# Rotary score passes of two heads on 64 rows each, and the order of copies around them, in a latent-attention layer on one NeuronCore

## Chip, cores and metric

The kernel runs on one core of a Trainium2 chip. The metric is the device time of one execution in microseconds (us); lower is better. Everything is computed in float32: each operand of a matmul is split into a high part (rounded to the matmul's format, `fp32r`) and a low part (what is left), and a product is made of hi x hi, hi x lo and lo x hi.

## What is computed

One decoder layer: multi-head latent attention, a residual with LayerNorm, a squared-ReLU MLP, and a second residual with LayerNorm. There are 512 tokens of width 2048, 16 heads, 128 plain and 64 rotary dimensions of queries and keys, 128 of values. The part that matters here:

```python
cq, ckv, k_rope = split(x @ w_in)                # 512, 512 and 64 wide
q = (rms_norm(cq) @ w_uq).reshape(B, S, 16, 128 + 64)
kv = (rms_norm(ckv) @ w_ukv).reshape(B, S, 16, 128 + 128)
q_rope, k_rope = apply_rope(q_rope), apply_rope(k_rope)   # one k_rope for all heads
s = (q_nope @ k_nope.T + q_rope @ k_rope.T) * 192 ** -0.5
p = softmax(where(causal, s, -inf))              # 128-query blocks
h = layer_norm(ALPHA * x + (p @ v) @ w_o)
```

## The kernel before

Every engine has its own instruction stream, written out by hand in a function of its own; semaphores tie them together, and the order within a stream is the order of the code. There is no scheduler. The stages follow one another: the input projection (up to 110 us of the trace), attention (to about 372), the output projection by Strassen-like products (to about 500), LayerNorm, and the MLP.

Attention goes by pairs of heads, `attention(pair, ahead)`, eight times; pair 0 and the last ones stand apart, the others run in a loop on each engine. While a pair's scores become probabilities, TensorE makes the projections of the next pair (`ahead`). For one pair TensorE runs: `scores` of head 0 and of head 1; `query` of the next pair's two heads and `rope_query`, the rotary queries of both heads (12 matmuls of 512 columns each); `transpose_probs` of head 0; `key` 0; `transpose_probs` of head 1; `key` 1 and `value` 0; `weigh_values` of both heads; `value` 1. The last pair has no next one: in place of the three projections stand `first_o_products`, 18 matmuls of the output projection.

`scores(pair, h)` makes, for each of four query blocks `t`, the scores against the 128 (t + 1) keys up to it, in the three banks of PSUM of head `h` (banks 0 to 2 for head 0, 3 to 5 for head 1). Five passes each: three of the plain part (`product`), then rotary with the key's high part (`kr_hi`), then with its low part (`kr_lo`). `qr[:, h, :]` holds the high part of head `h`'s rotary queries in 64 partitions (the first half for head 0, the second for head 1) and their low part in the other 64; `kr_hi` holds the key's high part in both halves, so that one pass adds hi x hi and lo x hi. `kr_lo[:, h, :]` holds the low part of the key in the half of head `h` and zeros in the other.

VectorE: `maxima` waits for a head's scores (`scored`), adds the causal mask, takes the row maxima and negates them; `normalise` divides by the sums; `query`, `key` and `values` make the low parts of the projections; `head_parts_lo` (L1536) makes `o_lo`, the low parts of the previous pair's seven sums of head outputs; `rope_query` rotates; `prob_t_los` makes the low parts of the transposed probabilities. ScalarE: `exps`, the copies out of PSUM that make the high parts (`q_hi`, `k_hi`, `v_hi`, `pt_hi`, `qr`), the swap of the rotary halves (`rope_swap`, L796), and `weights`, the high part of a block of weights. GpSimd makes the low part of that block (L666). A pair has four blocks of weights, held in four slots; each goes through one of two raw buffers, and SyncE loads a raw buffer when the low part of the block two before is made (L407).

The bank that `query(pair + 1, 0)` writes (6) is also that of `rope_query(pair + 1)`, which therefore waits until VectorE has made `q_lo` of head 0. `key(pair + 1, 0)` writes the bank of `query(pair + 1, 1)`.

Of the kernel before, what the change touches and what calls it, by code (L numbers as in the profile page):

```python
# [4 lines left out]
P = 128  # L5
D = 2048
S = 512
KD = D // P
TT = S // P
# [15 lines left out]
QKV_HB = 4  # L25
HB_QKV = IN_HB
# [66 lines left out]
KB = 1024  # L93
# [56 lines left out]
def mla_mlp_program(nc, xT, x, w, w_out, w_up, w_down, const, gain, ln, out):  # L150
# [3 lines left out]
    with ExitStack() as ctx:  # L154
# [33 lines left out]
        kr_hi, kr_lo = sb("kr_hi", [P, S], f32r), sb("kr_lo", [P, 2, S], f32r)  # L188
        place[0] += 2 * KB
# [547 lines left out]
        def _(act):  # L737
# [96 lines left out]
            def rope_query(pair, stream=True):  # L834
                if stream:
                    weights(HB_QKV + QKV_HB, pair)
                rope_swap(pair + 1, rope_bank(pair))

            def rope_query_hi(pair):
                act.wait_ge(rope_rotated, pair + 2)  # L840
                for half, h in zip(halves, range(2)):
                    last = act.activation(qr[half, h, :], rot[half, :], ACT.Copy)
                last.then_inc(rope_hi, 1)

# [68 lines left out]
            def attention(pair, ahead, stream=True):  # L913

                behind = not (isinstance(pair, int) and pair == 0)
                if behind:
                    head_parts_hi(pair - 1)
                    store_heads(pair - 1, 0)
                exps(pair, 0)
                if ahead:  # L920
                    query(pair + 1, 0)
                exps(pair, 1)
                if ahead:
                    query(pair + 1, 1)
                    rope_query(pair + 1, stream)
                else:
                    o_weights(0, 2)
                prob_t_his(pair, 0)
                if ahead:
                    key(pair + 1, 0)  # L930
                    rope_query_hi(pair + 1)
                else:
                    store_heads(pair - 1, 1)
# [408 lines left out]
        def _(dve):  # L1342
# [64 lines left out]
            for h in range(2):  # L1407
                last = dve.memset(kr_lo[64 - 64 * h:128 - 64 * h, h, :].bitcast(f32), 0.0)
            last.then_inc(ones_made, 1)
# [53 lines left out]
            def key_rope_lo():  # L1463
                dve.wait_ge(rope_hi, 1)
                dve.wait_ge(ones_made, 2)
                for half, h in zip(halves, range(2)):
                    last = dve.tensor_tensor(kr_lo[half, h, :], rot[half, :], kr_hi[half, :].bitcast(f32), ALU.subtract)
                last.then_inc(rope_split, 1)
# [122 lines left out]
            def attention(pair, ahead):  # L1591

                behind = not (isinstance(pair, int) and pair == 0)
                maxima(pair, 0)
                maxima(pair, 1)
                normalise(pair, 0)
                if ahead:
                    query(pair + 1, 0)
                else:
                    head_parts_lo(pair - 1)  # L1600
                normalise(pair, 1)
                if ahead:
                    query(pair + 1, 1)
                    if behind:
                        head_parts_lo(pair - 1)
                    rope_query(pair + 1)
                    key(pair + 1, 0)
# [564 lines left out]
        def _(pe):  # L2172
# [158 lines left out]

            def scores(pair, h):
# [5 lines left out]
                for t in range(TT):  # L2338
                    q, keys = slice(P * t, P * t + P), slice(0, P * (t + 1))
                    dst = score_bank(h)[:, SCORE_AT[t]:SCORE_AT[t] + P * (t + 1)]  # L2340
                    product(dst, q_hi[:, h, q], q_lo[:, h, q], k_hi[:, h, keys], k_lo[:, h, keys], True, False)

                    pe.matmul(dst, qr[:, h, q], kr_hi[:, keys], start=False, stop=False)  # L2343

                    last = pe.matmul(dst, qr[:, h, q], kr_lo[:, h, keys], start=False, stop=True)  # L2345
                last.then_inc(scored, 1)
# [48 lines left out]
            def attention(pair, ahead):  # L2395
                scores(pair, 0)
                scores(pair, 1)
                if ahead:
# [401 lines left out]
```

## Time and profile before

| | |
|---|---|
| runs | 1809.42, 1809.54, 1810.21 us; median 1809.54 |
| profiled execution | 1809.06 us, of which the span of its instructions is 1807.3 us |
| TensorE busy | 1784.9 us (99%), at a granted clock of 0.998 |
| VectorE busy | 1536.6 us (85%) |
| ScalarE busy | 944.2 us (52%) |
| GpSimd busy | 181.3 us (10%) |

Rows of a timeline read: start in us, duration in us, engine (PE is TensorE's matmuls, DVE VectorE, ACT ScalarE, POOL GpSimd), line, instruction, output<-inputs, and shapes, the output's first; `x4` is a merged group, and in square brackets stands the idle time of the engine ahead of it with what ended it. Matmuls are pipelined: one lasts longer than the distance to the next, and it is the distance that counts.

### The profile page before, as it was taken

Reading aid. Unit: us, or ns where it says so; the run is one execution under the profiler, and the core shown is the slowest. Engines: PE = TensorE matmul, PEld = TensorE weight load, DVE = VectorE, ACT = ScalarE, POOL = GpSimd, SP = SyncE. Lnnn points to the kernel's source line nnn. Section 1 sums busy time; section 2 is a strip of 40 time slices with the busy share of each in tenths; the row PEclk is TensorE's granted clock in tenths of the full one; section 3 lists DMA queues with packets and bytes.
Section 4 is the critical chain, followed back from the end, with each engine's and each line's share of the span. In section 5 each row is a group of like instructions: output and inputs, shape, how many; then the busy total and the mean of one; then the engine's idle time right before and its main releaser. Section 6 shows DMA issues by size and latency. Waiting matters only on the chain.

```text
span 1807.3 us, 26399 instructions
## 1 busy us (share of the span) xinstructions
PE 1784.9 (99%) x9996; PEld 1560.8 (86%) x9996; DVE 1536.6 (85%) x1865; ACT 944.2 (52%) x1191; POOL 181.3 (10%) x100
## 2 busy tenths in 40 slices
PE   9999999999999999999999999999999999999997
PEld 7888988978889999999999999988888888888886
DVE  4167777699999999999999999899989999989986
ACT  5256666553456666666666666643333334333342
POOL 3353323000020000000000000000011111100003
PEclk9999999999999999999999999999999999999999
DMA  6222433598224765566556656688465474754832
GB/s 236 82 102 90 135 119 119 202 351 304 92 88 171 232 214 193 186 206 214 178 194 211 205 174 205 241 308 325 154 266 202 188 281 157 279 195 164 311 117 93
DMA packets 131734, 351.77 MB, mean 195 GB/s; under 512 B 7632, under 2 KB 80208, under 8 KB 113232
## 3 DMA queue, kind: packets, MB, share of 16 engines
q1 hardware_dynamic: 57264, 275.67, 41.1%
q10 hardware_dynamic: 74400, 75.26, 13.4%
q8 instruction: 33, 0.54, 0.1%
q14 instruction: 37, 0.30, 0.0%
HBM read 268.59 MB, written 82.31 MB: 194 GB/s over the span
## 4 chain that ended last, share of the span: by engine, by line
PE 92%; DVE 5%; DMA 1%; issue 1%; ACT 1%; ACTq 0%; DVEq 0%; SPq 0%
PE bank L2183 24%; PE bank L2187 24%; PE bank L2188 24%; PE bank L2507 12%; PE bank L2511 6%; DVE w_lo L1549 1%; PE bank L2353 1%; DMA o_b<-out_weights 1%; PE bank L2345 0%; PE bank L2343 0%; DVE small L1504 0%; DMA first_raw<-weights 0%; DVE small L1659 0%; DVE up_both L1755 0%; DVE o_lo L1541 0%
## 5 line engine op out<-in xcount | busy, mean ns | idle before, releaser
L1264 ACT ACTIVATE w_hi<-d_b 128x1024 fp32r<-128x1024 f32 x180 | 189.4, 1060 | 299.0 <-PE bank L2188 239.4
L2183 PE MATMUL bank<-w_hi,down_act 128*128 128x512 f32 x864 | 336.6, 390 | 0.4 <-issue 0.4
L2188 PE MATMUL bank<-w_hi,down_act 128*128 128x512 f32 x864 | 336.2, 389 | 0.0
L2187 PE MATMUL bank<-w_lo,down_act 128*128 128x512 f32 x864 | 336.2, 389 | 0.0
L2507 PE MATMUL bank<-up_both,w_hi 128*128 128x512 f32 x896 | 321.1, 397 | 0.0
L2183 PE MATMUL bank<-up_both,w_hi 128*128 128x256 f32 x912 | 258.2, 283 | 0.6 <-issue 0.4
L2187 PE MATMUL bank<-up_both,w_hi 128*128 128x256 f32 x912 | 258.0, 283 | 0.0
L2188 PE MATMUL bank<-up_both,w_lo 128*128 128x256 f32 x912 | 257.9, 283 | 0.0
L1919 DVE TENSOR_TENSOR w_lo<-d_b,w_hi 128x1024 fp32r<-128x1024 f32 x180 | 214.7, 1226 | 23.9 <-ACT w_hi L1264 23.9
L2511 PE MATMUL bank<-up_both,w_lo 128*128 128x256 f32 x896 | 233.3, 281 | 0.0
L1768 DVE TENSOR_TENSOR w_lo<-up_b,w_hi 128x1024 fp32r<-128x1024 f32 x180 | 216.9, 1218 | 10.3 <-ACT w_hi L1009 10.3
L1009 ACT ACTIVATE w_hi<-up_b 128x1024 fp32r<-128x1024 f32 x180 | 186.8, 1054 | 31.9 <-PE bank L2188 31.9
L2507 PEld LDWEIGHTS bank<-up_both,w_hi 128*128 128x128 f32 x896 | 166.6, 188 | 30.7
L2183 PEld LDWEIGHTS bank<-w_hi,down_act 128*128 128x128 f32 x864 | 162.2, 188 | 35.7 <-issue 1.5
L2188 PEld LDWEIGHTS bank<-w_hi,down_act 128*128 128x128 f32 x864 | 162.2, 188 | 33.8
L2187 PEld LDWEIGHTS bank<-w_lo,down_act 128*128 128x128 f32 x864 | 162.2, 188 | 33.5
L2187 PEld LDWEIGHTS bank<-up_both,w_hi 128*128 128x128 f32 x912 | 173.2, 190 | 3.8
L2511 PEld LDWEIGHTS bank<-up_both,w_lo 128*128 128x128 f32 x896 | 169.2, 189 | 6.4
L2183 PEld LDWEIGHTS bank<-up_both,w_hi 128*128 128x128 f32 x912 | 173.2, 190 | 1.3 <-issue 1.0
L2188 PEld LDWEIGHTS bank<-up_both,w_lo 128*128 128x128 f32 x912 | 173.2, 190 | 0.0
L1979 DVE TENSOR_TENSOR acc<-acc,bank 128x512 f32<-128x512 f32 x194 | 126.0, 679 | 25.1 <-PE bank L2188 24.8
L666 POOL TENSOR_TENSOR w_lo<-raw,w_hi 128x1024 fp32r<-128x1024 f32 x46 | 112.0, 2438 | 213.2 <-ACT w_hi L744 213.0
(225 smaller groups left out, 3236.5 us busy)
## 6 DMA issues: line engine op xcount, KB each, us to landing
up_b<-up_weights SPq DMA_DIRECT2D x128, 512.0 KB, 4.4
d_b<-down_weights SPq DMA_DIRECT2D x64, 1024.0 KB, 5.2
down_act<-acts_kept SPq DMA_DIRECT2D x56, 1024.0 KB, 5.0
acts_kept<-h_hi ACTq DMA_DIRECT2D x32, 896.0 KB, 4.2
acts_kept<-h_lo ACTq DMA_DIRECT2D x32, 896.0 KB, 5.5
raw<-weights SPq DMA_DIRECT2D x46, 512.0 KB, 3.2
o_b<-out_weights SPq DMA_DIRECT2D x16, 1024.0 KB, 7.7
o_act<-o_kept SPq DMA_DIRECT2D x13, 1024.0 KB, 9.1
```

Source lines behind the costliest of these rows:

```text
L666: pool.tensor_tensor(w_lo[:, s, :], raw[:, s % RAWS, :], w_hi[:, s, :].bitcast(f32), ALU.subtract)\
L1009: act.activation(w_hi[:, UP_SLOT[u], :], source[:, :], ACT.Copy).then_inc(up_hi, 1)
L1264: act.activation(w_hi[:, DOWN_SLOT[n], :], source[:, ab, :], ACT.Copy).then_inc(down_hi, 1)
L1549: dve.tensor_tensor(w_lo[:, O_SLOT[n], :], source[:, ab, :], w_hi[:, O_SLOT[n], :].bitcast(f32), ALU.subtract).then_inc(made, 1)
L1768: dve.tensor_tensor(w_lo[:, s, :], source[:, :], w_hi[:, s, :].bitcast(f32), ALU.subtract).then_inc(up_lo, 1)
L1919: dve.tensor_tensor(w_lo[:, DOWN_SLOT[n], :], source[:, ab, :], w_hi[:, DOWN_SLOT[n], :].bitcast(f32), ALU.subtract).then_inc(made, 1)
L1979: dve.tensor_tensor(part, part, of, ALU.add).then_inc(evicted, 1)
L2183: first_pass = pe.matmul(out_, a_hi, b_hi, start=start, stop=False, skip_group_check=more)
L2187: pe.matmul(out_, a_hi, b_lo, start=False, stop=False, skip_group_check=more)
L2188: return pe.matmul(out_, a_lo, b_hi, start=False, stop=stop, skip_group_check=more)
L2507: return pe.matmul(dst, w_hi[:, s, P * k:P * k + P], up_both[left][:, :, k, :], start=u == 0 and k == 0, stop=k == HK - 1, skip_group_chec ...
L2511: return pe.matmul(dst[:, 0:HT], w_lo[:, s, P * k:P * k + P], up_act[left][0][:, k, :], start=False, stop=False, skip_group_check=True)
```

## The change

1. `kr_lo` loses its second plane and its zeros (two memsets of VectorE, and a wait for them). Both halves hold the key's low part, made by one subtraction over 128 partitions in place of two over 64.
2. `scores` leaves out the low-key pass. A new function, `score_lows`, runs after the scores of both heads: for each `t`, one matmul for head 0 on rows 0 to 63 of the array and one for head 1 on rows 64 to 127, between the 64 partitions of `qr` with the high part and those of `kr_lo`. The signal `scored` of both heads comes from the last two of these.
3. ScalarE copies `q_hi` of the next pair's head 0 ahead of the exponentials of head 0, and that of head 1 ahead of those of head 1. VectorE makes the low parts ahead of `maxima` of head 1 and ahead of `normalise` of head 1.
4. ScalarE's `rope_swap` no longer stands behind a block of weights; that block is made behind the copies of `qr`.
5. VectorE makes `o_lo` ahead of the maxima of head 0, in place of behind the second `q_lo` (in the last pair: between the two `normalise`).

```diff
-        kr_hi, kr_lo = sb("kr_hi", [P, S], f32r), sb("kr_lo", [P, 2, S], f32r)
-        place[0] += 2 * KB
+        kr_hi, kr_lo = sb("kr_hi", [P, S], f32r), sb("kr_lo", [P, S], f32r)
+        place[0] += 4 * KB
...
-            def rope_query(pair, stream=True):
-                if stream:
-                    weights(HB_QKV + QKV_HB, pair)
+            def rope_query(pair):
                 rope_swap(pair + 1, rope_bank(pair))
 
-            def rope_query_hi(pair):
+            def rope_query_hi(pair, stream=True):
                 act.wait_ge(rope_rotated, pair + 2)
                 for half, h in zip(halves, range(2)):
                     last = act.activation(qr[half, h, :], rot[half, :], ACT.Copy)
                 last.then_inc(rope_hi, 1)
+                if stream:
+                    weights(HB_QKV + QKV_HB, pair)
...
+                if ahead:
+                    query(pair + 1, 0)
                 exps(pair, 0)
                 if ahead:
-                    query(pair + 1, 0)
+                    query(pair + 1, 1)
                 exps(pair, 1)
                 if ahead:
-                    query(pair + 1, 1)
-                    rope_query(pair + 1, stream)
+                    rope_query(pair + 1)
...
-            for h in range(2):
-                last = dve.memset(kr_lo[64 - 64 * h:128 - 64 * h, h, :].bitcast(f32), 0.0)
-            last.then_inc(ones_made, 1)
...
-                dve.wait_ge(ones_made, 2)
-                for half, h in zip(halves, range(2)):
-                    last = dve.tensor_tensor(kr_lo[half, h, :], rot[half, :], kr_hi[half, :].bitcast(f32), ALU.subtract)
-                last.then_inc(rope_split, 1)
+                dve.tensor_tensor(kr_lo[:, :], rot[:, :], kr_hi[:, :].bitcast(f32), ALU.subtract).then_inc(rope_split, 1)
...
+                if behind:
+                    head_parts_lo(pair - 1)
                 maxima(pair, 0)
+                if ahead:
+                    query(pair + 1, 0)
                 maxima(pair, 1)
                 normalise(pair, 0)
                 if ahead:
-                    query(pair + 1, 0)
-                else:
-                    head_parts_lo(pair - 1)
+                    query(pair + 1, 1)
                 normalise(pair, 1)
                 if ahead:
-                    query(pair + 1, 1)
-                    if behind:
-                        head_parts_lo(pair - 1)
                     rope_query(pair + 1)
...
+            def score_block(h, t):
+                return score_bank(h)[:, SCORE_AT[t]:SCORE_AT[t] + P * (t + 1)]
+
...
-                    dst = score_bank(h)[:, SCORE_AT[t]:SCORE_AT[t] + P * (t + 1)]
-                    product(dst, q_hi[:, h, q], q_lo[:, h, q], k_hi[:, h, keys], k_lo[:, h, keys], True, False)
-
-                    pe.matmul(dst, qr[:, h, q], kr_hi[:, keys], start=False, stop=False)
-
-                    last = pe.matmul(dst, qr[:, h, q], kr_lo[:, h, keys], start=False, stop=True)
-                last.then_inc(scored, 1)
+                    product(score_block(h, t), q_hi[:, h, q], q_lo[:, h, q], k_hi[:, h, keys], k_lo[:, h, keys], t != 2, False, t == 2)
+
+                    pe.matmul(score_block(h, t), qr[:, h, q], kr_hi[:, keys], start=False, stop=False,
+                              skip_group_check=t == 2)
+
+            def score_lows():
+
+
+                for t in range(TT):
+                    q, keys = slice(P * t, P * t + P), slice(0, P * (t + 1))
+                    for half, h in zip(halves, range(2)):
+                        last = pe.matmul(score_block(h, t), qr[half, h, q], kr_lo[half, keys], start=False, stop=True,
+                                         skip_group_check=t == 2, tile_position=(64 * h, 0))
+                        if t == TT - 1:
+                            last.then_inc(scored, 1)
...
                 scores(pair, 1)
+                score_lows()
                 if ahead:
                     query(pair + 1, 0)
```

How the streams stand then. TensorE, the end of a pair's scores; before, where the next projection begins with the last row:

```order
L2343 MATMUL bank<-kr_hi,qr 128x384
L2345 MATMUL bank<-kr_lo,qr 128x384
L2183 MATMUL bank<-k_hi,q_hi 128x512
L2187 MATMUL bank<-k_lo,q_hi 128x512
L2188 MATMUL bank<-k_hi,q_lo 128x512
L2343 MATMUL bank<-kr_hi,qr 128x512
L2345 MATMUL bank<-kr_lo,qr 128x512
L2183 MATMUL bank<-mid_hi,w_hi 128x512
```

and now:

```order
L2339 MATMUL bank<-kr_hi,qr 128x384
L2177 MATMUL bank<-k_hi,q_hi 128x512
L2181 MATMUL bank<-k_lo,q_hi 128x512
L2182 MATMUL bank<-k_hi,q_lo 128x512
L2339 MATMUL bank<-kr_hi,qr 128x512
L2348 MATMUL bank<-kr_lo,qr 128x128 x2
L2348 MATMUL bank<-kr_lo,qr 128x256 x2
L2348 MATMUL bank<-kr_lo,qr 128x384 x2
L2348 MATMUL bank<-kr_lo,qr 128x512 x2
L2177 MATMUL bank<-mid_hi,w_hi 128x512
```

The low passes of both heads have moved from within the scores to their end, two of a width side by side.

VectorE, from the end of one pair to the maxima of the next; `small` holds the maxima, `bank<-bank,table` is the mask. Before:

```order
L1472 TENSOR_TENSOR v_lo<-bank,v_hi 128x512
L1499 TENSOR_TENSOR bank<-bank,table 128x2x2x128
L1504 TENSOR_REDUCE small<-bank 128x1 x4
L1507 TENSOR_SCALAR small<-small 128x4
L1499 TENSOR_TENSOR bank<-bank,table 128x2x2x128
L1504 TENSOR_REDUCE small<-bank 128x1 x4
L1507 TENSOR_SCALAR small<-small 128x4
L1511 RECIPROCAL small<-small 128x4
```

and now:

```order
L1467 TENSOR_TENSOR v_lo<-bank,v_hi 128x512
L1536 TENSOR_TENSOR o_lo<-o_raw,o_hi 128x1792
L1494 TENSOR_TENSOR bank<-bank,table 128x2x2x128
L1499 TENSOR_REDUCE small<-bank 128x1 x4
L1502 TENSOR_SCALAR small<-small 128x4
L1467 TENSOR_TENSOR q_lo<-bank,q_hi 128x512
L1494 TENSOR_TENSOR bank<-bank,table 128x2x2x128
L1499 TENSOR_REDUCE small<-bank 128x1 x4
L1502 TENSOR_SCALAR small<-small 128x4
L1506 RECIPROCAL small<-small 128x4
```

`o_lo` stands ahead of the first mask and `q_lo` of head 0 between the two heads' maxima.

ScalarE, from the exponentials of head 1 on. Before:

```order
L829 ACTIVATE q_hi<-bank 128x512
L744 ACTIVATE w_hi<-raw 128x1024
L802 ACTIVATE swap<-bank 32x512 x4
L869 ACTIVATE pt_hi<-bank 128x512
L869 ACTIVATE pt_hi<-bank 128x768
L829 ACTIVATE k_hi<-bank 128x512
L842 ACTIVATE qr<-rot 64x512 x2
L869 ACTIVATE pt_hi<-bank 128x512
L869 ACTIVATE pt_hi<-bank 128x768
L744 ACTIVATE w_hi<-raw 128x1024
L829 ACTIVATE k_hi<-bank 128x512
L744 ACTIVATE w_hi<-raw 128x1024
```

and now:

```order
L802 ACTIVATE swap<-bank 32x512 x4
L869 ACTIVATE pt_hi<-bank 128x512
L869 ACTIVATE pt_hi<-bank 128x768
L829 ACTIVATE k_hi<-bank 128x512
L840 ACTIVATE qr<-rot 64x512 x2
L744 ACTIVATE w_hi<-raw 128x1024
L869 ACTIVATE pt_hi<-bank 128x512
L869 ACTIVATE pt_hi<-bank 128x768
L744 ACTIVATE w_hi<-raw 128x1024
L829 ACTIVATE k_hi<-bank 128x512
L744 ACTIVATE w_hi<-raw 128x1024
```

The first block of weights (`w_hi`) has gone from ahead of the swaps to behind `qr`.

## Rows read from the trace of the kernel before

**Rows 1.** The page, its first part: busy us, share of the span, instructions

```profile
PE 1784.9 (99%) x9996; PEld 1560.8 (86%) x9996; DVE 1536.6 (85%) x1865; ACT 944.2 (52%) x1191; POOL 181.3 (10%) x100
```

**Rows 2.** Windows: stretch, its length, busy time of each engine, clock, DMA

```profile
277.20:309.00 31.80, 31.80 (x195) 28.60 (x194) 23.27 (x43) 20.46 (x39) 9.61 (x4) 1.00 0.37 124
```

**Rows 3.** Timeline of TensorE, the scores of pair 5

```profile
290.01 0.27 PE L2345 MATMUL bank<-kr_lo,qr 128*128 128x128 f32 x1
290.12 0.34 PE L2183 MATMUL bank<-k_hi,q_hi 128*128 128x256 f32 x1
...
290.64 0.28 PE L2345 MATMUL bank<-kr_lo,qr 128*128 128x256 f32 x1
290.76 0.34 PE L2183 MATMUL bank<-k_hi,q_hi 128*128 128x384 f32 x1
...
291.46 0.33 PE L2345 MATMUL bank<-kr_lo,qr 128*128 128x384 f32 x1
291.64 0.39 PE L2183 MATMUL bank<-k_hi,q_hi 128*128 128x512 f32 x1
...
292.56 0.39 PE L2345 MATMUL bank<-kr_lo,qr 128*128 128x512 f32 x1
292.79 0.22 PE L2183 MATMUL bank<-k_hi,q_hi 128*128 128x128 f32 x1
...
295.96 0.40 PE L2183 MATMUL bank<-mid_hi,w_hi 128*128 128x512 f32 x1
```

**Rows 4.** Timeline of TensorE: transposes of pair 5, and after the wait in pair 0

```profile
304.15 1.25 PE L2353 MATMUL bank<-table,probs 128*128 128x128 f32 x10
305.16 0.48 PE L2183 MATMUL bank<-mid_hi,w_hi 128*128 128x512 f32 x1
...
142.27 0.50 PE L2183 MATMUL bank<-mid_hi,w_hi 128*128 128x512 f32 x1 [0.67 <-DVE q_lo L1472]
```

**Rows 5.** Timeline of VectorE, pair 5

```profile
296.16 0.70 DVE L1499 TENSOR_TENSOR bank<-bank,table 128x512 f32<-128x512 f32 x1 [0.56 <-PE bank L2345]
...
298.90 1.28 DVE L1515 TENSOR_SCALAR probs<-probs,small 128x128 f32<-128x128 f32 x4
...
303.57 3.93 DVE L1541 TENSOR_TENSOR o_lo<-o_raw,o_hi 128x1792 fp32r<-128x1792 f32 x1
```

**Rows 6.** Timeline of ScalarE, pair 5

```profile
298.90 0.60 ACT L829 ACTIVATE q_hi<-bank 128x512 fp32r<-128x512 f32 x1 [1.12 <-PE bank L2188]
...
304.43 2.40 ACT L802 ACTIVATE swap<-bank 32x512 f32<-32x512 f32 x4 [1.26 <-PE bank L2188]
```

**Rows 7.** Timeline of GpSimd, pair 5

```profile
303.25 2.38 POOL L666 TENSOR_TENSOR w_lo<-raw,w_hi 128x1024 fp32r<-128x1024 f32 x1 [9.41 <-ACT w_hi L744]
```

**Rows 8.** DMA issues from 150 to 340 us: KB each, median us to landing

```profile
raw<-weights SPq DMA_DIRECT2D x21, 512.0 KB, 3.2
```

**Rows 9.** Timelines of VectorE and ScalarE, pair 0

```profile
135.45 2.25 DVE L1507 TENSOR_SCALAR small<-small 128x4 f32<-128x4 f32 x1
...
135.22 1.28 ACT L862 ACT_TABLE_LOAD   x1
```

**Rows 10.** Timelines of ScalarE, VectorE and TensorE, the last pair

```profile
355.95 1.68 ACT L885 ACTIVATE o_hi<-o_raw 128x1792 fp32r<-128x1792 f32 x1
...
357.41 0.69 DVE L1499 TENSOR_TENSOR bank<-bank,table 128x512 f32<-128x512 f32 x1
...
362.65 1.27 DVE L1515 TENSOR_SCALAR probs<-probs,small 128x128 f32<-128x128 f32 x4
363.84 2.02 DVE L1541 TENSOR_TENSOR o_lo<-o_raw,o_hi 128x1792 fp32r<-128x1792 f32 x1
...
363.99 1.31 PE L2353 MATMUL bank<-table,probs 128*128 128x128 f32 x10 [0.16 <-DVE probs L1515]
...
371.38 0.50 PE L2183 MATMUL bank<-pt_hi,v_hi 128*128 128x512 f32 x1 [0.40 <-DVE pt_lo L1522]
```

**Rows 11.** Timeline of ScalarE, the output stage

```profile
408.81 2.01 ACT L911 ACTIVATE w_hi<-o_b 128x1024 fp32r<-128x1024 f32 x2 [3.00 <-DMA o_b<-out_weights]
```

More of the change, by code:

```diff
@@ L930, in attention @@
                     key(pair + 1, 0)
-                    rope_query_hi(pair + 1)
+                    rope_query_hi(pair + 1, stream)
                 else:
```

## The prediction

> **What bounds the kernel now.** I read the page's first part, then the busy time of one period of the attention stage, then the timelines of TensorE, VectorE, ScalarE and GpSimd through one steady pair of heads, and through the first and the last pair. TensorE works for 1784.9 of 1807.3 us [rows 1]. The edits lie in the attention stage (118 to 372 us). A steady pair takes 31.80 us, all of it TensorE's, with VectorE busy 23.3 and ScalarE 20.5 [rows 2]. So time taken from TensorE is gained in full, and a later partner costs only what exceeds TensorE's need. The profiled execution took 1809.06 us, 0.48 under the median of the runs (1809.54). The sum is made against the former and 0.5 us is added at the end. A difference under 0.2% (3.6 us) can't be told from none.
>
> **The low-key passes.** Each matmul's price is the start of the next less its own: 0.11 us at 128 columns, 0.12 at 256, 0.18 at 384, 0.23 at 512 [rows 3]. Four widths make 0.64 us a head, 1.27 a pair of heads; a head's twenty passes take 3.17 (292.79 to 295.96). The change keeps eight matmuls a pair, each on 64 rows of the array, those of the two heads on different rows and into different banks of PSUM. The trace of before has no 64-row matmul, so their cost has bounds only. Lowest: both heads of a width run at once and cost one, 0.64. Highest: no overlap, 1.27. Between: at 128 and 256 columns the pace is about 0.115 for either width, though the columns double; so it is a weight load, not the columns, that paces them. If the loads stay one after another, eight cost 8 x 0.115 = 0.92, with the columns hidden. I take 0.92, since it is the row nearest to what is kept: eight weight loads.
>
> To this come two changes of the array's form a pair, into 64 rows and out. Nearest row: after ten transposes the first wide matmul shows 0.48 instead of 0.39, so 0.09. Upper bound: a fully emptied array, where the first matmul after a wait shows 0.50 instead of 0.39 (0.11), and the tail of the one before is exposed (0.39 long at 0.23 spacing, 0.16): 0.27 [rows 4]. Two make 0.16 to 0.54; I take 0.16. So a pair costs 0.92 + 0.16 = 1.08 in place of 1.27, 0.19 gained, with ends at +0.47 (0.80) and -0.54 (1.81). For pairs 0 to 6, a **gain of 1.3 us**; pair 7 is separate.
>
> The rows price a change of form only by relatives. The Trainium skill, "TensorEngine Tiling (Array Packing)", Key Properties, speaks on both sides: tiles load weights and multiply independently of each other, and changing the mode drains TensorE. No trace here shows either yet. As an estimate by that page, full overlap with two drains at the row's 0.27 is 0.64 + 0.54 = 1.18, and the end 0.7 us later than mine.
>
> **The first transposes become tight.** Before, head 0's scores were released at once and its maxima ran under head 1's passes, some 3 us ahead (after 292.79, where those of head 1 ran after 295.96) [rows 3]. Now both heads are released by the last two low passes. Call the end of the scores E. TensorE then runs three projections and wants the transposes at E + 8.19 (295.96 to 304.15) [rows 3, 4]. VectorE's chain: masking and maxima of head 0 end at about E + 2.8. First query projection ends at E + 2.73; ScalarE copies it from 0.2 later for 0.6 (295.96 + 2.73 = 298.69, q_hi at 298.90 for 0.60) [rows 3, 6], so q_lo starts at E + 3.56 and takes 0.61. Mask of head 1 to the start of its normalising is 2.74 (296.16 to 298.90, with the same instructions between) [rows 5], normalising 1.28: E + 8.19, and 0.07 to the transposes (at 363.99, after a normalising from 362.65 to 363.92) [rows 10]. The exponentials of head 0 (E + 3.4 to 5.6) are hidden. So TensorE waits some 0.07, and 0.05 with weights not fetched ahead: 0.1 us a pair, a **loss of 0.7 us**. Of this 4.1 us slack of before nothing is left, and each further 0.1 us costs 0.7. Head 1's transposes keep about 1.5 us, the second query's low part 0.3, the key's wait on the rotation 0.9. The early copy is what makes this possible: q_lo frees the bank that the rotary projection writes at E + 5.4; left behind head 1's normalising it would come at E + 8.
>
> **The moved low parts of heads.** o_lo took 3.93 us at 303.57 while GpSimd ran from 303.25 to 305.63 [rows 5, 7], but 2.02 in the last pair, where GpSimd is idle [rows 10]: it waits for GpSimd's end, then takes 1.9. At its new place it starts when o_hi is there, 3.3 us into the scores, waits for the fourth block's subtraction (it ends at 4.2) and ends near 6.1; the scores end near 6.2. VectorE has nothing else to do there, and until q_hi comes it has 0.75 us more of room. Costed at nothing. The Trainium skill, "SBUF — State Buffer", Who interferes with whom, has the rule, a VectorE instruction with two SBUF inputs and a GpSimd one that reads SBUF exclude each other; the trace agrees, 3.93 against 2.02.
>
> **The moved weight block.** Its ScalarE copy, which released GpSimd at 303.25 [rows 7], goes from ahead of the swaps to behind qr, E + 14.8, and GpSimd's 2.4 us to E + 18.2 with it. Before, swaps waited for the projection 1.26 us anyway [rows 6], so nothing is gained on TensorE. The block two further uses the same raw buffer: its transfer (SyncE waits for the subtraction) lands 3.2 us later [rows 8], E + 21.6, while ScalarE wants it at E + 18.6. ScalarE will wait 3 us there, ahead of the copies of the heads' outputs. Those are wanted by the next scores at E + 25.3, and come at 23.2 and 23.9. Hidden, with 2 us of room; nothing.
>
> **The first pair.** GpSimd held the negated maximum, 2.25 us instead of 0.17 [rows 9], and so TensorE stood at 142.27 for 0.67, 0.9 with the restart [rows 4]. With maxima 2.6 us later the negation comes when GpSimd is through. Against it, the exponentials' table load of 1.28 (135.22, hidden before) now stands behind the first query copy: 0.3 late. Net **gain 0.6**.
>
> **The last pair.** No projections follow its scores, but 4.1 us of output products. VectorE must first make o_lo: o_hi ends at 357.63, o_lo at about 359.6, and masking starts there instead of at 357.41 [rows 10], so the transposes come near 366.2, not 363.99, and TensorE stands about 3 us. Part comes back, since o_lo no longer stands between the normalisings and three small waits of TensorE shrink: VectorE's added idle time is 0.25 ahead of o_lo, 0.8 for head 1's exponentials, 0.2 at pt_hi, and head 1's value product starts near 372.7, not 371.38 [rows 10]. **Loss 1.3**, whatever the low passes cost. The output stage behind is VectorE's and the DMA's: at 408.81 ScalarE had waited 3.00 us for weights [rows 11]. Its burst of loads begins on the store of o_lo, 1.6 us later by ScalarE's queue against 1.3 for the engines: **loss 0.3** (0 to 2).
>
> The removed zeroing and the joined kr_lo lie where TensorE never waits: nothing. Sum: -1.3 + 0.7 - 0.6 + 1.3 + 0.3 = +0.4: 1809.5, as a median 1809.9.
>
> **Rivals.** *Full overlap*: 0.64, or 0.80 with the cheap changes of form. The gain is 4.4 or 3.3 in place of 1.3: 1806.8 to 1807.9, say 1807.3. For it speaks that heads share neither rows nor banks; against it the weight-load pace. *No overlap* (the matmuls don't do what the change says): 1.43 to 1.81 a pair, a loss of 1.1 to 3.8: 1812.3 to 1815.0. It is slower from about 1.6 a pair on. *o_lo meets GpSimd*: if the fourth block's subtraction starts just ahead of o_lo instead of 1.5 us earlier, o_lo is held 2.4 us; 0.75 are free, 1.5 in six pairs reach the first transposes, +9: 1819. The order within a pair puts them 1.5 us apart; it decides when the third block's transfer takes over some 6 us, which pushes the fourth block back. The 3.2 of [rows 8] speaks against it.
>
> **Chances.** Forecast (1808.5 to 1811.5) 0.5, full overlap 0.2, no overlap 0.17, o_lo late 0.05, the rest, above all transposes 0.2 to 0.4 us later than worked out (1811 to 1813), 0.08. The range goes from below full overlap, 1806.3, to 1813.5 in the middle of no overlap. Faster by over 0.2% (under 1805.9) needs full overlap and the last pair's loss away: 0.06; slower (over 1813.2): 0.16; same 0.78.
>
> **What would show it.** Spacing of the 64-row matmuls: about 0.11 from each to the next is mine, pairs a few ns apart with 0.11 to 0.23 between pairs is full overlap, full widths in line is none. The period of a steady pair: 31.7 expected, 31.3 or 32.3 for the rivals. A small wait of the first transposes for VectorE in each pair, over 2 us in the last; none at 142 us. VectorE waiting for head 0's release, with o_lo in 2.5 to 3 us. ScalarE waiting about 3 us for raw weights each pair. If transposes wait over 0.3 us in steady pairs, my chain is wrong; if the last pair loses under 1 us, that term is.

## The result, and the profile after

| | before | after |
|---|---|---|
| median of six runs each | 1810.13 us (1809.42 to 1810.71) | 1822.59 us (1821.03 to 1823.80) |
| profiled execution | 1809.06 us, span 1807.3 | 1821.03 us, span 1819.2 |

The ratio is 1.0067, interval 1.0057 to 1.0078: slower, by over 0.2%. The forecast was 1809.9 us with a range of 1806.3 to 1813.5, so it missed, and by far: the changed kernel loses about 12.5 us where +0.4 was expected.

The first part of the changed kernel's profile page, which answers to [rows 1]:

```profile
PE 1787.9 (98%) x9996; PEld 1557.7 (86%) x9996; DVE 1537.9 (85%) x1862; ACT 942.8 (52%) x1191; POOL 184.7 (10%) x100
```

TensorE is busy for 3.0 us more than before, of 11.9 that the span grew: most of the loss is standing. The waits of TensorE by what ended them (us in total, times, the longest) name it:

```profile
PE bank L2177 <- DVE q_lo L1467: 8.5, 1, 8.5
PE bank L2358 <- DVE probs L1510: 2.8, 2, 2.6
```

The first is one wait of 8.5 us, once in the whole kernel; the longest of the second line is 2.6 us. The starts of the pairs (first matmul of `scores`) say where:

| period of pair | 0 | 1 to 5 | 6 |
|---|---|---|---|
| before | 32.79 | 31.80 each | 31.80 |
| after | 32.33 | 31.78, 31.84, 31.86, 31.87, 31.85 | 41.77 |

Five steady pairs are as long as before within 0.07 us; pair 6 alone is 9.97 us longer. Up to the MLP's first block of weights on ScalarE (510.84 before, 521.38 after) the loss is 10.54: 9.97 in pair 6, 0.20 in pairs 1 to 5, 1.33 in the last pair to its second value product, less 0.46 in pair 0, 0.13 ahead of it and 0.37 in the output stage. The other 1.4 us of the span come in the MLP, in which nothing is changed; there the experiments' profiled executions differ from the one before by -0.3 to +2.0 us. So the marks of the attention stage decide below, and the medians beside them.

**What happened in pair 6.** The chain of waits from 320 to 345 us (start, duration, what) goes back to a transfer:

```profile
317.64 16.37 DMA o_kept<-o_lo
...
334.10 1.70 ACT o_hi L885
...
337.87 0.70 DVE bank L1494
...
338.59 1.70 DVE small L1499 x4
...
340.44 0.70 DVE q_lo L1467
...
341.26 0.79 PE bank L2177
342.05 0.43 PE bank L2181
```

The store of `o_lo`, the low parts of the heads' outputs, takes 16.37 us to land. `head_parts_hi` of the next pair would overwrite `o_hi`, and it waits for both stores of the pair before by one semaphore (`o_stored`). Behind `o_hi` on VectorE stand `o_lo`, now ahead of the maxima, then the maxima and `q_lo` of head 0, and for that one TensorE waits.

Why the store is so slow is in two timelines. ScalarE's, where `ACTq` is the issue of a DMA on its queue:

```profile
317.49 1.06 ACT L744 ACTIVATE w_hi<-raw 128x1024 fp32r<-128x1024 f32 x1 [3.58 <-DMA raw<-weights]
317.64 0.38 ACTq L891 DMA_DIRECT2D o_kept<-o_lo  x1
...
334.10 1.70 ACT L885 ACTIVATE o_hi<-o_raw 128x1792 fp32r<-128x1792 f32 x1 [11.33 <-DMA o_kept<-o_lo]
```

and SyncE's, after the last two raw blocks of weights:

```profile
317.48 0.34 SPq L430 DMA_DIRECT2D o_b<-out_weights  x1
317.87 2.02 SPq L433 DMA_DIRECT2D o_act<-o_kept  x3
```

The same places before:

```profile
312.36 0.38 ACTq L891 DMA_DIRECT2D o_kept<-o_lo  x1
...
316.42 0.34 SPq L430 DMA_DIRECT2D o_b<-out_weights  x1
316.81 2.05 SPq L433 DMA_DIRECT2D o_act<-o_kept  x3
```

The store (896 KB) is issued behind the third block's `w_hi`. Before, it left 4.1 us ahead of four loads of 1 MB each, the first of the output stage. After, it leaves 5.3 us later, since `w_hi` waits 3.58 us for raw weights, and stands between the loads. They come once, in pair 5. One pair earlier the store leaves as late (285.82, in pair 4), and the next `o_hi` waits 0.22 us for it.

**The low passes.** TensorE's timeline over the end of the scores of pair 5; the second and third fence are narrower windows, and so show the merged group from its second width on (x6) and its last (x2):

```profile
294.03 0.39 PE L2339 MATMUL bank<-kr_hi,qr 128*128 128x512 f32 x1
294.35 0.91 PE L2348 MATMUL bank<-kr_lo,qr 64*128 64x128 f32 x8
295.18 0.51 PE L2177 MATMUL bank<-mid_hi,w_hi 128*128 128x512 f32 x1
295.53 0.39 PE L2181 MATMUL bank<-mid_lo,w_hi 128*128 128x512 f32 x1
```

```profile
294.51 0.74 PE L2348 MATMUL bank<-kr_lo,qr 64*128 64x256 f32 x6
```

```profile
294.86 0.40 PE L2348 MATMUL bank<-kr_lo,qr 64*128 64x512 f32 x2
```

The two matmuls of a width start together: 294.35, 294.51, 294.68, 294.86. The eight take 0.83 us; going in costs 0.09 (294.03 to 294.35 is 0.32, not 0.23), coming out 0.12 (295.18 to 295.53 is 0.35). From 294.03 to 295.53 are 1.50 us, less two wide matmuls at 0.23: 1.04, against 1.27 before. The Trainium skill, "TensorEngine Tiling (Array Packing)", Key Properties, says that tiles load their weights and multiply independently and that a change of mode drains TensorE. The trace agrees with the first: the matmuls of the two heads, each with weights of its own, start together. For the second it has 0.09 us lost going in and 0.12 coming out, as a drain would show; no row shows the drain itself.

**Why steady pairs gain nothing.** The 0.23 go at two places. The first transposes start 0.05 late, just behind the normalising of head 0, which ends at 303.49, and show the restart (303.54, wanted at 303.49; the next wide matmul is 0.06 later behind them than before): 0.11. The value product of head 1 starts 1.98 us behind that of head 0 (314.16, 316.14), before 1.85 (314.71, 316.56), which is 0.13, and 0.03 follow: 0.16. Timelines of VectorE and GpSimd there, after:

```profile
310.99 3.51 DVE L1478 TENSOR_TENSOR qr<-rot,qr 64x512 fp32r<-64x512 f32 x2
314.53 1.55 DVE L1517 TENSOR_TENSOR pt_lo<-bank,pt_hi 128x512 fp32r<-128x512 f32 x2
```

```profile
311.37 5.39 POOL L666 TENSOR_TENSOR w_lo<-raw,w_hi 128x1024 fp32r<-128x1024 f32 x2 [17.97 <-ACT w_hi L744]
```

and VectorE's before:

```profile
311.59 1.39 DVE L1483 TENSOR_TENSOR qr<-rot,qr 64x512 fp32r<-64x512 f32 x2
```

The moved block's subtraction on GpSimd now meets VectorE's `qr`, 3.51 us in place of 1.39. Sum of a steady pair: -0.23 + 0.11 + 0.16 = +0.04; the starts show +0.05 (pair 5). Pair 6 bears this out where it isn't stalled (the experiments on the early store and on the later burst): it makes no new blocks of weights, so nothing holds `qr`, and it takes 31.68, which is 31.80 - 0.23 + 0.11.

**The last pair**, TensorE's timeline; its first transposes answer to the row at 363.99 of [rows 10]:

```profile
375.77 1.31 PE L2358 MATMUL bank<-table,probs 128*128 128x128 f32 x10 [2.59 <-DVE probs L1510]
...
382.29 0.50 PE L2177 MATMUL bank<-pt_hi,v_hi 128*128 128x512 f32 x1 [0.40 <-DVE pt_lo L1517]
```

### The profile page after: what moved, and what is told of

The parts are those of the page before. It is cut to its first block, busy times and chain, and to the rows that moved or that the text cites. A ratio compares the mean times of both kernels' runs of the same rounds, so it can differ in the third digit from the quotient of the medians.

```text
span 1819.2 us, 26400 instructions
## 1 busy us (share of the span) xinstructions
PE 1787.9 (98%) x9996; PEld 1557.7 (86%) x9996; DVE 1537.9 (85%) x1862; ACT 942.8 (52%) x1191; POOL 184.7 (10%) x100
## 4 chain that ended last, share of the span: by engine, by line
PE 74%; issue 12%; POOL 5%; DVE 5%; DMA 2%; ACT 1%; SPq 0%; POOLq 0%; DVEq 0%; ACTq 0%
PE bank L2177 19%; PE bank L2181 19%; PE bank L2182 19%; PE bank L2513 12%; PE bank L2517 6%; POOL w_lo L666 5%; DMA o_kept<-o_lo 1%; DVE w_lo L1913 1%; DMA d_b<-down_weights 1%; DMA x_raw<-x_t 1%; DVE small L1499 0%; DVE small L1653 0%; DVE d_b L1948 0%; DVE acc L1970 0%; DVE w_lo L1544 0%
```

## The experiments

Theory A, formed on this profile: the moved block delays the store of `o_lo` into the burst of loads, and that is the loss; the rest of the change is about even. Theory B: the moved `o_lo` or the late maxima are to blame on their own, and the store is beside the point.

### The store issued earlier

```diff
                 exps(pair, 1)
                 if ahead:
+                    if behind:
+                        store_heads(pair - 1, 1)
                     rope_query(pair + 1)
...
                     key(pair + 1, 1, stream)
-                    if behind:
-                        store_heads(pair - 1, 1)
```

> The changed kernel, with the store of the previous pair's o_lo issued on ScalarE's queue behind the exponentials of head 1 (ahead of the rotary swaps), and not behind the third block of weights. Theory A: in the changed kernel ScalarE waits for the raw buffer of the third block, the store of o_lo behind it goes out at 317.6 us in place of 312.4, meets four loads of 1 MB that SyncE issues at 317.5 to 319, takes 16 us, and o_hi of the next pair waits 11 us for it, with the copy of the next queries and the maxima behind it; TensorE stands 8.5 us once and runs 3 us at half clock: 10 us in all. Then here that goes: 1811 to 1812.5 (10 to 12 us less than the changed kernel), no wait of o_hi, no low clock. Theory B (o_lo ahead of the maxima is what stalls, whatever the store does): 1820 to 1823, the stall stays.

Measured: 1812.14 us, ratio 1.0012 (1.0003 to 1.0022). ScalarE, then SyncE:

```profile
302.93 0.38 ACTq L891 DMA_DIRECT2D o_kept<-o_lo  x1
...
323.30 1.69 ACT L885 ACTIVATE o_hi<-o_raw 128x1792 fp32r<-128x1792 f32 x1
```

```profile
318.12 0.34 SPq L430 DMA_DIRECT2D o_b<-out_weights  x1
318.51 2.13 SPq L433 DMA_DIRECT2D o_act<-o_kept  x3
```

The store leaves at 302.93, `o_hi` starts at 323.30 without a wait, and pair 6 takes 31.68 us, while SyncE's burst is where it was (318.12 to 320.64). One line of order was worth 10 us. What is left of the loss is the last pair, below.

### The block of weights moved back

In the changed kernel, item 4 alone undone.

```diff
-            def rope_query(pair):
+            def rope_query(pair, stream=True):
+                if stream:
+                    weights(HB_QKV + QKV_HB, pair)
...
-            def rope_query_hi(pair, stream=True):
+            def rope_query_hi(pair):
...
-                if stream:
-                    weights(HB_QKV + QKV_HB, pair)
```

> The changed kernel, with the moved block of weights back ahead of the rotary swaps; the store of o_lo stays where it is, behind the third block. Theory A: the third block no longer waits for its buffer, the store goes out at about 312, and the stall is gone; also qr's low part no longer meets GpSimd and the value product of head 1 no longer waits (0.16 us a pair): 1810.5 to 1812. Swaps come 1 us later, which just fits. Theory B: the stall stays, 1820 or more.

Measured: 1814.85 us, 1.0027 (1.0018 to 1.0037). The stall in pair 6 is gone (it takes 31.68), but steady pairs take 32.34 us, so the 1810.5 to 1812 of theory A was wrong. TensorE and VectorE in pair 1:

```profile
181.49 1.31 PE L2358 MATMUL bank<-table,probs 128*128 128x128 f32 x10 [0.42 <-DVE probs L1510]
```

```profile
177.98 3.46 DVE L1510 TENSOR_SCALAR probs<-probs,small 128x128 f32<-128x128 f32 x4
```

The normalising of head 1, later now since the maxima are, meets GpSimd's subtraction, which starts at 178.76, with the last of its four instructions (178.77), and the four take 3.46 us in place of 1.28. So the move has a use that the prediction did not see, 0.5 us a pair (32.34 against 31.85). The Trainium skill, "SBUF — State Buffer", Who interferes with whom, says that a VectorE instruction with two SBUF inputs contends with a GpSimd one that reads SBUF, and that a `tensor_scalar` in a two-port mode does too. `qr` is of the first kind, and the trace agrees, 3.51 us against 1.39. The normalising is a `tensor_scalar`, 3.46 against 1.28; that it runs in such a mode no row shows.

### The block alone, in the kernel before

The same edit the other way round, with nothing else of the change.

```diff
-            def rope_query(pair, stream=True):
-                if stream:
-                    weights(HB_QKV + QKV_HB, pair)
+            def rope_query(pair):
...
-            def rope_query_hi(pair):
+            def rope_query_hi(pair, stream=True):
...
+                if stream:
+                    weights(HB_QKV + QKV_HB, pair)
```

> The kernel before, with one part of the change alone: the block of weights moved from ahead of the rotary swaps to behind the copies of qr. Theory A: the stall comes with this part alone, since the store goes out late here too and o_hi stands ahead of the exponentials in both kernels: 8 to 11 us more than before, 1818 to 1821, with 0.1 to 0.2 us a pair for the value product of head 1. Theory B (the stall needs o_lo ahead of the maxima, or the late release of the scores): 1809 to 1811.

Measured: 1820.09 us, 1.0057 (1.0040 to 1.0073). Pair 6 takes 41.90. Steady pairs stay at 31.80, so the 0.1 to 0.2 us a pair expected for the value product did not come: `qr` is held here too (3.51 us from 311.99), but the second value product starts 1.86 us behind the first (315.57, 317.43), as before. The hold costs TensorE something only where the rest of the pair has become shorter. ScalarE, then TensorE:

```profile
318.57 0.39 ACTq L891 DMA_DIRECT2D o_kept<-o_lo  x1
...
335.09 1.70 ACT L885 ACTIVATE o_hi<-o_raw 128x1792 fp32r<-128x1792 f32 x1 [11.07 <-DMA o_kept<-o_lo]
```

```profile
341.65 0.79 PE L2183 MATMUL bank<-mid_hi,w_hi 128*128 128x512 f32 x1 [7.40 <-DVE q_lo L1472]
```

The stall needs neither the early copies nor the moved `o_lo`: theory B falls. Here `o_lo` stands behind the maxima, and TensorE waits nearly as long: `o_hi` itself holds ScalarE, and with it `exps` and `q_hi`.

### The burst issued later

In the changed kernel, SyncE's wait ahead of the burst.

```diff
-            sp.wait_ge(o_stored, 32 * CK)
+            sp.wait_ge(o_stored, 32 * CK + 32)
```

> The changed kernel, with SyncE's first loads of the output stage (one of weights, three of kept heads, 1 MB each) waiting for the stores of one pair more, so that they go out when the late store of o_lo has landed. ScalarE's queue is as in the changed kernel. Theory A says the store takes 16 us since it shares the DMA engines with these loads: alone it takes 4 to 6 us (317.6 to about 323), o_hi waits under 1 us, the stall is gone: 1811 to 1813.5. Rival (the store is merely late; 5 us of delay are enough): a stall of several us stays, 1818 or more.

Measured: 1811.19 us, 1.0007 (0.9998 to 1.0017). The store leaves as late as in the changed kernel, but alone:

```profile
318.24 0.38 ACTq L891 DMA_DIRECT2D o_kept<-o_lo  x1
...
323.69 1.71 ACT L885 ACTIVATE o_hi<-o_raw 128x1792 fp32r<-128x1792 f32 x1 [0.32 <-DMA o_kept<-o_lo]
```

It lands within 5.45 us, in place of 16.37. Both halves of theory A are shown: a late store without the burst costs nothing (pair 6 takes 31.68 here too), nor does the burst with an early store. How the loads hold the store up, no run shows.

### Full rows for the low passes

This experiment and all that follow are made on top of the early store. The eight passes stay at the end of the scores, on 128 rows, with the zeros in `kr_lo`; the products are the same.

```diff
-                        last = pe.matmul(score_block(h, t), qr[half, h, q], kr_lo[half, keys], start=False, stop=True,
-                                         skip_group_check=t == 2, tile_position=(64 * h, 0))
+                        last = pe.matmul(score_block(h, t), qr[:, h, q], kr_lo[:, h, keys], start=False, stop=True,
+                                         skip_group_check=t == 2)
```

> As e1_store_early, but the low-key passes at the end of the scores use all 128 rows again (kr_lo with zeros in the other head's half, as in the kernel before). This measures the 64-row form by itself. The trace of the changed kernel shows two 64-row matmuls starting together and the next two 0.16, 0.17 and 0.18 us later, 0.83 for the eight, with 0.09 lost ahead of them and 0.12 behind: 1.04 a pair against 1.27. Theory A (that is their whole effect): a steady pair takes 0.23 us more than in e1_store_early (32.08 in place of 31.85), the whole 1.6 to 1.8 us more. Theory B (the changes of form cost more elsewhere): no difference, or this one faster.

Measured: 1813.51 us, 1.0019 (1.0009 to 1.0028); steady pairs 32.10 where the early store alone has 31.85. The passes take 1.27 us (295.96 to 297.23). So 64 rows are worth 0.25 us a pair by the period, 0.23 by the spacing. From the first pair to the start of the last it is 1.66 us; the medians lie 1.4 apart, a little under the 1.6 to 1.8 expected and within their spread.

### The early copies undone

```diff
-                if ahead:
-                    query(pair + 1, 0)
                 exps(pair, 0)
                 if ahead:
-                    query(pair + 1, 1)
+                    query(pair + 1, 0)
                 exps(pair, 1)
                 if ahead:
+                    query(pair + 1, 1)
```

(on ScalarE; on VectorE likewise, each `q_lo` back behind a `normalise`)

> As e1_store_early, but the copies of the next queries and their low parts stand where the kernel before had them (behind the exponentials of head 0 and 1; behind the normalising of head 0 and 1). Theory A (the prediction's step): q_lo of head 0 comes at 7.4 us behind the end of the scores where TensorE's rotary projection wants it at 5.45: TensorE waits 2 us in each of seven pairs, 13 to 15 us in all, 1824 to 1828, more if the clock falls. Theory B (the early copies do not matter): 1811 to 1813.

Measured: 1822.54 us, 1.0072 (1.0056 to 1.0087), below the 1824 to 1828 expected; 33.52 a pair, 1.67 more, with TensorE waiting each time:

```profile
310.77 0.49 PE L2175 MATMUL bank<-mid_hi,w_hi 128*128 128x512 f32 x1 [1.65 <-DVE q_lo L1466]
```

The place is the one expected, the rotary projection's bank; the size of the wait was put 0.3 us too high in each of seven pairs. With the low passes at the end, the early copies are needed.

### The last pair in the old order

`score_lows` is called for each head behind its own scores in the last pair, and `o_lo` goes back between the two `normalise` there.

```diff
             def attention(pair, ahead):
                 scores(pair, 0)
+                if not ahead:
+                    score_lows((0,))
                 scores(pair, 1)
-                score_lows()
+                score_lows() if ahead else score_lows((1,))
...
-                if behind:
+                if behind and ahead:
                     head_parts_lo(pair - 1)
...
                     query(pair + 1, 1)
+                else:
+                    head_parts_lo(pair - 1)
```

> As e1_store_early, with the last pair in the old order: the 64-row low passes of head 0 right behind its scores, those of head 1 behind its own, and o_lo between the two normalisings. Theory A: TensorE's wait of 2.6 us at the last pair's first transposes goes, and with it the low clock behind it in some executions; two more changes of form and passes that no longer run at once cost 0.5. 1809 to 1810.5, 1.5 to 3 us under e1_store_early, and a narrower spread of the executions. Theory B (the output stage behind it swallows the difference): no change from e1_store_early.

Measured: 1809.89 us, 0.9999 (0.9989 to 1.0008). The MLP's first block is at 510.80, in the kernel before at 510.84 and with the early store alone at 513.27. So the last pair's loss, some 2.3 us in that execution with the early store, is gone. The spread that was expected to narrow is 1808.6 to 1811.3 here, 1809.9 to 1813.9 with the early store, and 1808.8 to 1813.1 for the kernel before in the same rounds: that shows nothing either way.

### The block of weights one step later

On top of the last pair's old order, the moved block goes behind `pt_hi` of head 1, to keep its subtraction off `qr`.

```diff
-                    rope_query_hi(pair + 1, stream)
+                    rope_query_hi(pair + 1)
...
                 prob_t_his(pair, 1)
                 if ahead:
+                    next_block(pair + 1, stream)
                     key(pair + 1, 1, stream)
```

(`next_block` is the call of `weights` that stood in `rope_query_hi`)

> As e7_last_pair, with the moved block of weights one step later, behind pt_hi of head 1 and not behind the copies of qr. Theory A: in the changed kernel the second half of qr's low part waits 2.1 us for GpSimd's subtraction of this block (3.51 us in place of 1.39), pt_lo of head 1 comes late by that, and the value product of head 1 waits 0.16 us in each of six pairs. Here that goes: a steady pair takes 31.68 in place of 31.85, in all 1.0 us less than e7_last_pair, 1808 to 1809.5, a little under the kernel before. Theory B (the third block's transfer, later too, delays the heads' outputs past the next scores): steady pairs longer.

Measured: 1817.19 us, 1.0038 (1.0024 to 1.0052): a miss for the expected gain. `qr` takes 1.39 us again, but pairs 1 to 6 take 32.9 to 33.4. ScalarE, then VectorE:

```profile
325.30 1.06 ACT L744 ACTIVATE w_hi<-raw 128x1024 fp32r<-128x1024 f32 x1 [4.59 <-DMA raw<-weights]
```

```profile
329.84 2.50 DVE L1533 TENSOR_TENSOR o_raw<-o_raw 128x256 f32<-128x256 f32 x1
```

Each time that the block is put off, the delay comes back at the next use of its raw buffer: 4.59 us of waiting, ahead of the heads' outputs. Their sums come late and meet GpSimd's next subtraction (2.50 us; the two of the same shape just ahead of it take 0.41 each), and `o_hi`, `o_lo` and the maxima with them. The copies of the heads' outputs, which the prediction gave 2 us of room, end at 319.52 in the changed kernel, 1.5 us ahead of the next scores (321.02), and at 327.33 here, 0.24 ahead of them (327.57); what comes late is the work behind them.

### `qr` behind the key's low part

Again on top of the last pair's old order. Instead of the block, the instruction that it holds up is moved.

```diff
                 prob_t_los(pair, 0)
-                if ahead:
-                    rope_query_lo(pair + 1)
-                else:
+                if not ahead:
                     o_rest_part(0, 1, 0)
                 prob_t_los(pair, 1)
                 if ahead:
                     key(pair + 1, 1)
+                    rope_query_lo(pair + 1)
```

> As e7_last_pair, and VectorE makes qr's low part behind pt_lo and k_lo of head 1, not ahead of them; ScalarE and GpSimd keep their order. Theory A: the value product of head 1 waits 0.16 us in steady pairs since pt_lo stands behind qr's low part, which GpSimd holds up. With qr's low part behind, nobody waits for it before the next scores, 5 us later: a steady pair takes 31.68 to 31.70 in place of 31.85, the whole about 1 us less than e7_last_pair, 1808 to 1809.5, at or just under the kernel before (0 to 0.1%). Theory B (the value product waits for something else): steady pairs stay at 31.85.

Measured: 1809.18 us, 0.9994 (0.9985 to 1.0003). Steady pairs take 31.70, 0.15 less than without the edit and 0.10 less than the kernel before; the second value product starts 1.85 us behind the first again (314.04, 315.89). `qr` is still held (2.74 us), where nobody waits for it. The MLP's first block is at 510.15. This is the fastest of all, and a measurement can't tell it from the kernel before.

## Why the prediction was wrong

**The failed step is "the moved weight block", costed at nothing.** Its working was right as far as it went: ScalarE's wait for raw weights was put at 3 us and is 3.6, and the copies of the heads' outputs bore it. But it named as queued behind that wait only ScalarE's copies. The issue of the `o_lo` store stands there too, and the next `o_hi` waits for its landing. What the runs showed in its place: the store left 5.3 us later, between four loads of 1 MB, and took 16.37 us to land; `o_hi` waited 11.33 us, TensorE 8.48, and pair 6 took 9.97 us more. With the store ahead of that wait, or with the loads behind the store, this is gone. The prediction had looked at what the block's transfers do to others, not at what others' transfers do to a store that leaves 5 us later. Nor did it look for the one place in the loop that differs from the rest: the last raw load, behind which SyncE issues the output stage's first 4 MB. The trace of before had a row on what these loads do: the store of `o_hi` issued at 324.77, behind them, took 8.5 us to land, where that of the pair before (293.10) took 4.8; nobody waited for it. Every rival spoke of a steady pair, times six or seven; this loss comes once, so no rival and no end of the range held it. The rival that named a time near the measured one, `o_lo` against GpSimd (1819), did not happen: `o_lo` took 2.3 us at its new place and ended as worked out. With 9.97 us added to the sum of +0.4, the time would be some 1820, and 1822.6 was measured.

**The low passes**: 1.08 was taken for a pair and 1.04 measured, but that was luck. The eight weight loads were supposed to go one after another at 0.115; those of two heads go side by side, with 0.16 to 0.18 from pair to pair. The rival of full overlap was right on the mechanism and low on the size: 0.83 for the four widths, not 0.64, since they take 0.16, 0.17, 0.18 and 0.32 to the next start, where whole matmuls take 0.11, 0.12, 0.18 and 0.23. The 0.32 has 0.09 over its width, which may belong to the change of form behind it. The changes of form beside that took 0.09 and 0.12, for the 0.16 expected of both together.

**The first transposes**: 0.1 a pair expected, 0.11 measured. `o_lo` ended when it should (6.12 us into the scores, 6.1 expected), 0.11 behind the last score.

**Missing in the sum**: 0.16 a pair for `qr` against GpSimd. The text followed the block's subtraction to E + 18.2 (E is the end of the scores, 295.18 in pair 5), and did not ask which VectorE instruction runs then; it asked just that of `o_lo`. In the other direction it gave the move no use, and the block moved back shows one of 0.5 us a pair. With the transposes' 0.11, `qr` takes back the whole gain of the low passes: steady pairs at 31.85, not 31.7.

**The first pair**: gain 0.46 for 0.6; the wait at 142 us is gone, another of 0.23 is at the transposes. **The last pair**: 1.33 lost to its second value product, for 1.3; TensorE stands 2.59 us, for "about 3". **The output stage**: no loss of 0.3; the mark at the MLP's start comes 0.37 earlier against that value product than before.

That the rest of the change is about even with the kernel before, but for the last pair, is shown by the early store: 1812.14 us, and 1809.89 with the last pair in its old order.

## What to carry to other kernels

When an instruction is moved, write down everything that its engine issues behind the new wait, the DMA issues first, and for each who waits for it to land and what other transfers stand near its new time. Then look for the iteration in which a loop's surroundings differ (the last load of a stream, the first of the next stage): a steady period says nothing of it, and an order that is harmless in every other pair can cost 10 us in one. A GpSimd block moved off one VectorE instruction can land on another, as it did here on `qr` and, one step later, on a sum of the heads' outputs; name the new one.

## What the runs showed of the hardware

- Two 64-row matmuls on different rows start together, and so do the loads of their weights (two at 294.34 to 294.35, the next two at 294.45 to 294.46); four pairs of 128 to 512 columns took 0.83 us, and the change of form 0.09 in and 0.12 out.
- A store of 896 KB took 16.4 us between four loads of 1 MB issued within 2.4 us, and under 5.5 us alone at the same place.
- TensorE's granted clock after a wait: it fell after both long waits (8.48, and 7.40 with the block alone moved), but after the last pair's wait, 2.34 to 2.59 us in six of the kernels, in three and not in the other three. In the changed kernel's profile it was 1.00 from 374 to 382 us, around the last pair's wait, and its ten transposes took 1.31 us. With the early store alone it fell to 0.84 and 0.73 around and behind the same wait, and the same ten took 2.04:

```profile
364.00:368.00 4.00, 1.69 (x10) 1.69 (x11) 3.07 (x12) 3.62 (x11) 0.00 (x0) 0.84 1.01 424
368.00:372.00 4.00, 4.00 (x20) 3.41 (x19) 3.35 (x5) 1.55 (x3) 0.00 (x0) 0.73 0.80 276
```

These are windows, the clock third from the end. After the wait of pair 6 in the changed kernel it was 0.50, the lower of the two levels (1.2 GHz), and wide matmuls followed one another by 0.43 us, not 0.23:

```profile
341.00:343.00 2.00, 1.74 (x4) 1.46 (x5) 1.97 (x6) 2.00 (x7) 0.00 (x0) 0.50 0.00 0
```

What decides it after the shorter wait stays open. From the last pair's start to the MLP the changed kernel lost 0.96 us on the kernel before (1.33 - 0.37). With the early store the last pair starts 0.13 later than before and the MLP 2.43: 2.30 lost, 1.3 more, in an execution where the clock fell. Whether this is behind the spread of 1809.9 to 1813.9 with the early store stays open: without the wait, in the last pair's old order, the executions spread over 2.8 us, those of the kernel before, which has no such wait either, over 4.3.
